# Spacing the tiles of the rounded operands by 2124 and 1100 bytes

## The chip, the cores and the metric

The kernel runs on one core of a Trainium2 chip. The metric is the device time of one launch in microseconds (us), taken as the median of several runs. A profile of one execution stands beside it. Its engines are PE (TensorE, matmuls), PEld (TensorE's loads of the stationary operand), DVE (VectorE), ACT (ScalarE), POOL (GpSimd) and SP (SyncE, which issues the transfers). A number such as L556 is a line of the kernel.

## The reference

For 256 tokens of width 1024 it computes, in float32, two blocks after each other. The first has two layers; each is

```
h = h + 0.5 * swiglu(rms_norm(h, g_ffn1), w_in, w_out)     # hidden width 2816
h = h + mixer(rms_norm(h, g_mix))                          # layer 0: latent attention, layer 1: attention with decay
h = h + 0.5 * swiglu(rms_norm(h, g_ffn2), w_in, w_out)
h = h + sigmoid(rms_norm(h, g_ple) @ w_gate) * (p @ w_proj)
```

with `swiglu(x) = (silu(gate) * up) @ w_out`. The second block is a projection `rms_norm(x) @ w_in` of 3592 columns, short convolutions and a gated delta rule, an output projection, and then 32 experts of width 512, two of them per token:

```
x = x + concat(y_a, y_b) @ w_out
x = x + hier_moe(rms_norm(x), ...)     # silu(x @ w_gate[e]) * (x @ w_up[e]) @ w_down[e]
return rms_norm(x)
```

## The kernel before

**Layout.** Activations lie feature-major: 128 features on the partitions, 8 tiles (`KD`) of 256 tokens. A matmul multiplies a stationary 128x128 tile by a moving operand of 256 or 512 columns into one of eight PSUM banks.

**Products in rounded parts.** TensorE takes plain float32 slowly, and a rounded float32 (`F32R`) faster. The large dense products therefore split both operands into a high part, rounded to `F32R`, and a low part, the rest, and add three products: high by high, low by high, high by low. The helper `three` (L570) does that for one tile. The input of a product lies in `x_parts` (L231): for each k of the 8 tiles the high part `x_hi[:, k]` and right behind it the low part `x_lo[:, k]`, 256 words each. Tile k + 1 follows tile k without a gap, so tiles begin every 2048 bytes. The gate output of a feed-forward layer lies in `act_hi`, `act_lo` and `act` (L236, L251, L252), two buffers each, 1024 bytes apart. The function `inside` (L200) makes these views. It lets all of them begin at word 15 (`INSIDE`) of a flat tensor that is 16 words (`LINE`) longer than it need be, that is at byte 60 of a group of 64; all later tiles begin at byte 60 of their group as well.

```
x_parts = inside(rounded_view("x_parts", [P, 2 * KD * T + LINE]), [P, KD, 2, T])
act_hi = inside(sb("act_hi", [P, 2 * T + LINE], F32R), [P, 2, T])
```

Some tensors share their bytes: `hn` and `sq` lie over `x_parts`, with `behind_hn` between them, `ring_lo` takes the bytes of `ring` itself, and the experts' ring `moe_ring` lies over both and what follows them.

**Weights.** They stream through a ring of four slots of 1.5 MB (`ring`), which SyncE fills in order as slots come free (`ring_free`). ScalarE writes the high parts into `high` or `high_first` (L1524), VectorE subtracts and writes the low parts to `ring_lo` (L2011). All these tiles begin at byte 0 of a group of 64.

**The feed-forward layer** (`gated`, L645, four times) takes 22 chunks of 128 hidden features. For a chunk, `gate_up` (L655) runs 16 matmuls of 512 columns, which take `x_parts[:, k]` whole, high and low side by side, under the high weights, first 8 for gate and then 8 for up; then 16 of 256 columns with `x_hi` under the low weights. `down` (L679) adds the chunk before to the output: 8 output tiles with three matmuls of 256 columns each on `act_hi` and `act_lo`; even chunks use buffer 0 and odd ones buffer 1. Meanwhile ScalarE and VectorE make the gate output of the present chunk (`act_part`, L2076) and split the weights of the next ones. The loop's order is written out by hand, with semaphores between engines.

**Elsewhere.** `x_high_pair` (L1531) and `x_low_pair` (L2037) write `x_hi` and `x_lo`. The second block's input projection (`mix_group`, L996, and the loop over k behind it) uses `three` with `x_hi` and `x_lo` in turn, 28 output tiles by 8. The token products of the attention with decay (`two_units`, L923) turn the roles: the weights move, 512 columns at a time, and `x_hi` and `x_lo` are stationary, 128 columns each. The experts use `act` through `slot_act` (L307), four slots of 128 words. Their weights come through `moe_ring`, twelve places of 1 MB; SyncE's first loads of them wait on `ring_free`, `mix_ready` and `lin_ready`, so for the last dense chunks. All dense matmuls are issued in the helper `mm` and stand under L556, the experts' under L1250.

Of the kernel before, what the change touches and what calls it, by code (L numbers as in the profile page):

```python
# [4 lines left out]


# [1 line left out]

# [1 line left out]

# [4 lines left out]
P = 128  # L15
T = 256
D = 1024
KD = D // P
# [13 lines left out]
QUAD = P // CAP  # L32
# [8 lines left out]
PIECES = 4  # L41
LINE = 16
INSIDE = 15
NEG = -1.0e30

F32 = mybir.dt.float32
F32R = mybir.dt.float32r
# [142 lines left out]
def two_block_kernel(nc, xT, pT, pos, par, weights, experts, out):  # L190
    with ExitStack() as ctx:
        def sb(name, shape, dt=F32):
            return ctx.enter_context(nc.sbuf_tensor("sb_" + name, shape, dt))

        def rounded_view(name, shape):

            with nc.sbuf_tensor("sb_" + name, shape, F32R) as view:
                return view

        def inside(flat, shape):  # L200

            n = math.prod(shape[1:])
            names = "abc"[:len(shape) - 1]
            dims = {a: shape[1 + i] for i, a in enumerate(names)}
            return flat[:, INSIDE:INSIDE + n].rearrange(f"p ({' '.join(names)}) -> p {' '.join(names)}", **dims)

        def sem(name):
            return ctx.enter_context(nc.semaphore(name))
# [2 lines left out]
        params = sb("params", [P, NPAR])  # L211
        narrow = sb("narrow", [P, 16])
        gq, eps_col, peak = narrow[:, 0:4], narrow[:, 4:5], narrow[:, 5:6].bitcast(I32)
        with nc.sbuf_tensor("sb_moe_ring", [P, MOE_RING, MCT * P], F32) as moe_ring:
            pass
        ring_lo = rounded_view("ring_lo", [P, RING, CT * P])
# [11 lines left out]
        v_tok = sb("v_tok", [P, 2, D])  # L228
        oT = sb("oT", [P, KD, T])
        h = sb("h", [P, KD, T])  # L230
        x_parts = inside(rounded_view("x_parts", [P, 2 * KD * T + LINE]), [P, KD, 2, T])  # L231
        x_hi, x_lo = x_parts[:, :, 0, :], x_parts[:, :, 1, :]
        hn = sb("hn", [P, KD, T])
        sb("behind_hn", [P, LINE])
        sq = sb("sq", [P, KD, T])
        act_hi = inside(sb("act_hi", [P, 2 * T + LINE], F32R), [P, 2, T])  # L236
        lnv = sb("lnv", [P, 2, 2 * T])
        rstd = sb("rstd", [P, 2, T])
        pin = sb("pin", [P, 2 * DEPTH, T])
# [8 lines left out]
            pass  # L248
        expg = sb("expg", [P, 2, T])
        gate_r = sb("gate_r", [P, 2, T])  # L250
        act_lo = inside(rounded_view("act_lo", [P, 2 * T + LINE]), [P, 2, T])  # L251
        act = inside(sb("act", [P, 2 * T + LINE]), [P, 2, T])  # L252
        sqh = sb("sqh", [P, 2, 2, T])
        rsh = sb("rsh", [P, 2, 2 * T])
        trig = sb("trig", [P, 4, 2, ROPE // 2])
# [50 lines left out]

        def slot_act(x):  # L307

            return act[:, :, :].rearrange("p a t -> p (a t)")[:, x % QUAD * P:(x % QUAD + 1) * P]
        partial = sq[:, 0:4, :].rearrange("p a t -> p (a t)").rearrange("p (b n) -> p b n", b=2)  # L310
        qkv_pad = scratch[:, 0:12 * PADQ].rearrange("p (n t) -> p n t", t=PADQ)
        u_pad = scratch[:, 12 * PADQ:12 * PADQ + 4 * PADU].rearrange("p (n t) -> p n t", t=PADU)
# [187 lines left out]
        def _(pool):  # L500
# [12 lines left out]
            for i in range(1 - QUAD, QUAD):  # L513
# [5 lines left out]

            st.link(nc.gpsimd.affine_select(out=mask, in_=mask, compare_op=ALU.is_ge, fill=NEG, base=0,  # L520
                                            pattern=[[-1, P]], channel_multiplier=1))
# [30 lines left out]
        def _(pe):  # L552
# [722 lines left out]
            def moe_gathered():  # L1275
# [40 lines left out]
                def down_half(r, p, h, at, pieces=False):  # L1316

                    pe.wait_ge(ex_act, r * QUAD + (2 * p + 2))
                    if not pieces:
                        for e in range(2):  # L1320
                            arrived(r, at + e)
                    for m in (2 * h, 2 * h + 1):
                        for half in range(2):
                            if pieces:
                                pe.wait_ge(last_in[2 * (m % 2) + half], 32)
                            for e in range(2):
                                x = 2 * p + e
                                expert_mm(B[4 + half][CAP * x:CAP * (x + 1), :], slot_act(x)[:, m * CAP:(m + 1) * CAP],
                                     four_tiles(at + e, 8 * (m % 2) + 4 * half), m == 0, m == EC - 1,
                                     (half_down if pieces and not half else ex_down if half else None)  # L1330
                                     if p and e and m == EC - 1 else None)
                    owed_moe[0] += 2
# [664 lines left out]
        def _(dve):  # L1997
# [695 lines left out]
            def R(lo, n):  # L2693
                return route[:, :, lo:lo + n]

            def wide(lo, n):
                return R(lo, 1).to_broadcast([P, 2, n])
# [7 lines left out]
            def by_group(lo):  # L2705
# [14 lines left out]
            V.tensor_tensor(R(40, 4), R(0, 4), wide(36, 4), ALU.subtract).then_inc(rt_max, 1)  # L2720
            st.link(V.scalar_tensor_tensor(out=R(224, 32), in0=R(128, 32), scalar=2.0 * NEG, in1=R(4, 32),
                                           op0=ALU.mult, op1=ALU.add))
# [51 lines left out]
            def moe_gathered():  # L2774
# [21 lines left out]
                def silu_up(r, x):  # L2796
                    s3_, a3 = (v.rearrange("p (m s) -> p m s", s=CAP) for v in (expg[:, 0, 0:P], slot_act(x)))
                    dve.wait_ge(ex_silu, r * QUAD + x + 1)
                    V.tensor_tensor(a3, turned_part(1), s3_, ALU.mult).then_inc(ex_act, 1)  # L2799
# [253 lines left out]
```

## Time and profile before

| | us |
|---|---|
| median of 3 runs | 1723.69 |
| lowest and highest | 1722.62 and 1724.35 |
| the profiled execution, its own time | 1723.16 |
| its span, first to last instruction | 1721.4 |
| TensorE busy | 1615.8 |
| VectorE busy | 987.8 |
| ScalarE busy | 610.3 |

The span is what the profile's views divide up; the execution's own time is 1.8 us longer. Dense products fill the first 1240 us or so, the experts the rest. TensorE's matmuls are pipelined: the busy time of one contains its way through the array, so the pace is the distance from one start to the next.

### The profile page before, as it was taken

Reading aid. Unit: us, or ns where it says so; the run is one execution under the profiler, and the core shown is the slowest. Engines: PE = TensorE matmul, PEld = TensorE weight load, DVE = VectorE, ACT = ScalarE, POOL = GpSimd, SP = SyncE. Lnnn points to the kernel's source line nnn. Section 1 sums busy time; section 2 is a strip of 40 time slices with the busy share of each in tenths; the row PEclk is TensorE's granted clock in tenths of the full one; section 3 lists DMA queues with packets and bytes.
Section 4 is the critical chain, followed back from the end, with each engine's and each line's share of the span. In section 5 each row is a group of like instructions: output and inputs, shape, how many; then the busy total and the mean of one; then the engine's idle time right before and its main releaser. Section 6 shows DMA issues by size and latency. Waiting matters only on the chain.

```text
span 1721.4 us, 25871 instructions
## 1 busy us (share of the span) xinstructions
PE 1615.8 (94%) x10376; PEld 1286.6 (75%) x10376; DVE 987.8 (57%) x1660; ACT 610.3 (35%) x809; POOL 56.4 (3%) x82
## 2 busy tenths in 40 slices
PE   6999999999999999999999999999989788778887
PEld 6999857899998999888889999999954344334333
DVE  7888655687867888865478885787331111111112
ACT  5333346434336333465443334653421000000001
POOL 3000005000000000001100000000000000000000
PEclk9999999999999999999999999999989999999999
DMA  7544441445554555544255555332689999999996
GB/s 279 192 185 183 184 183 74 184 183 190 198 232 158 198 196 184 198 153 164 74 199 200 186 184 220 118 141 74 258 373 425 427 427 427 428 427 427 428 427 271
DMA packets 49240, 415.65 MB, mean 241 GB/s; under 512 B 5616, under 2 KB 5648, under 8 KB 7824
## 3 DMA queue, kind: packets, MB, share of 16 engines
q1 hardware_dynamic: 49104, 414.61, 61.1%
q8 instruction: 51, 0.84, 0.2%
q14 instruction: 21, 0.17, 0.0%
q10 hardware_dynamic: 64, 0.03, 0.0%
HBM read 413.54 MB, written 1.05 MB: 241 GB/s over the span
## 4 chain that ended last, share of the span: by engine, by line
PE 73%; DMA 19%; DVE 4%; ACT 3%; issue 1%; SPq 0%; POOL 0%; DVEq 0%; ACTq 0%
PE bank L556 65%; DMA sb_moe_ring<-experts 18%; PE bank L1250 6%; DVE sb_ring_lo L2011 1%; ACT sb_high L1524 1%; DMA sb_ring<-weights 1%; PE bank L745 0%; PE bank L834 0%; DMA sb_h<-xT 0%; SPq L481 0%; DVE sb_x_parts L2040 0%; ACT sb_high_first L1524 0%; DVE sb_nmax L2144 0%; DVE sb_lnv L2047 0%; ACT sb_x_parts L1535 0%
## 5 line engine op out<-in xcount | busy, mean ns | idle before, releaser
L2011 DVE TENSOR_TENSOR sb_ring_lo<-sb_ring,sb_high 128x2304 fp32r<-128x2304 f32 (+4 forms) x180 | 351.9, 1956 | 123.4 <-ACT sb_high L1524 122.8
L556 PE MATMUL bank<-sb_x_parts,sb_high 128*128 128x512 f32 (+1 forms) x1792 | 407.5, 365 | 0.4 <-DVE sb_ring_lo L2011 0.2
L556 PEld LDWEIGHTS bank<-sb_x_parts,sb_high 128*128 128x128 f32 x1792 | 317.8, 189 | 49.5 <-DVE sb_ring_lo L2011 0.9
L1524 ACT ACTIVATE sb_high<-sb_ring 128x3072 fp32r<-128x3072 f32 x100 | 274.8, 2748 | 139.1 <-PE bank L556 111.0
L556 PE MATMUL bank<-sb_x_parts,sb_ring_lo 128*128 128x256 f32 x1632 | 253.0, 279 | 0.0
L556 PEld LDWEIGHTS bank<-sb_x_parts,sb_ring_lo 128*128 128x128 f32 x1632 | 224.5, 189 | 7.0
L556 PE MATMUL bank<-sb_act_hi,sb_ring_lo 128*128 128x256 f32 x704 | 195.0, 277 | 0.0
L556 PE MATMUL bank<-sb_act_hi,sb_high 128*128 128x256 f32 x680 | 188.6, 277 | 2.2 <-DVE sb_ring_lo L2011 1.7
L556 PE MATMUL bank<-sb_act_lo,sb_high 128*128 128x256 f32 x680 | 187.7, 276 | 0.0
L1250 PE MATMUL bank<-sb_moe_ring,sb_act 128*32 128x512 f32 x512 | 127.4, 643 | 41.2 <-DMA sb_moe_ring<-experts 41.1
L1566 ACT ACTIVATE sb_expg<-sb_gate_r 128x256 f32<-128x256 f32 x88 | 36.7, 417 | 338.0 <-DVE sb_gate_r L2074 337.9
L1250 PE MATMUL bank<-sb_moe_ring,sb_sq 128*32 128x512 f32 x984 | 119.9, 597 | 31.1 <-DMA sb_moe_ring<-experts 30.4
L556 PE MATMUL bank<-sb_oT,sb_ring 128*128 128x256 f32 x640 | 142.8, 379 | 0.0
L556 PEld LDWEIGHTS bank<-sb_oT,sb_ring 128*128 128x128 f32 x640 | 120.7, 190 | 16.7 <-issue 0.8
L556 PEld LDWEIGHTS bank<-sb_act_hi,sb_ring_lo 128*128 128x128 f32 x704 | 131.7, 187 | 0.0
L556 PEld LDWEIGHTS bank<-sb_act_hi,sb_high 128*128 128x128 f32 x680 | 127.2, 187 | 2.6 <-DVE sb_ring_lo L2011 1.9
L556 PEld LDWEIGHTS bank<-sb_act_lo,sb_high 128*128 128x128 f32 x680 | 127.2, 187 | 0.0
L1250 PEld LDWEIGHTS bank<-sb_moe_ring,sb_act 128*32 128x32 f32 x512 | 33.7, 117 | 119.3 <-issue 118.5
L2799 DVE TENSOR_TENSOR sb_act<-bank,sb_expg 128x128 f32<-128x128 f32 x32 | 9.3, 292 | 167.5 <-ACT sb_expg L1952 167.5
L1250 PEld LDWEIGHTS bank<-sb_moe_ring,sb_sq 128*32 128x32 f32 x984 | 28.8, 109 | 96.6 <-issue 92.9
L2794 DVE COPY sb_sq<-bank 128x512 f32<-128x512 f32 x32 | 22.1, 691 | 129.1 <-PE bank L1250 129.1
L1250 PEld LDWEIGHTS bank<-sb_stack,sb_sq 128*128 128x128 f32 x512 | 59.6, 191 | 29.4 <-issue 29.4
(385 smaller groups left out, 1894.5 us busy)
## 6 DMA issues: line engine op xcount, KB each, us to landing
sb_ring<-weights SPq DMA_DIRECT2D x133, 1536.0 KB, 6.5
sb_moe_ring<-experts SPq DMA_DIRECT2D x185, 1024.0 KB, 21.1
sb_qk<-experts SPq DMA_DIRECT2D x4, 1024.0 KB, 15.0
sb_moe_ring<-experts SPq DMA_DIRECT2D x8, 256.0 KB, 17.3
sb_h<-xT SPq DMA_DIRECT2D x2, 512.0 KB, 7.1
sb_ring<-weights SPq DMA_DIRECT2D x2, 512.0 KB, 7.8
sb_oT<-experts SPq DMA_DIRECT2D x1, 1024.0 KB, 15.4
sb_pin<-pT SPq DMA_DIRECT2D x1, 512.0 KB, 17.7
```

The source lines that it names most:

```text
L556: ins = nc.tensor.matmul(o, l, r, start=start, stop=stop, skip_group_check=True)
L1250: ins = nc.tensor.matmul(o, l, r, start=start, stop=stop, skip_group_check=True)
L1524: nc.scalar.activation(high_of(n)[:, lo * P:hi * P], ring[:, n % RING, lo * P:hi * P], ACT.Copy).then_inc(done, 1)
L1566: nc.scalar.activation(expg[:, b, :], gate_r[:, b, :], ACT.Silu).then_inc(sig_ready, 1)
L2011: return V.tensor_tensor(ring_lo[:, n % RING, cols], ring[:, n % RING, cols], high_of(n)[:, cols].bitcast(F32), ALU.subtract)
L2794: V.tensor_copy(partial[:, 1, :], B[1][:, :]).then_inc(part_in[1], 1)
L2799: V.tensor_tensor(a3, turned_part(1), s3_, ALU.mult).then_inc(ex_act, 1)
```

## The change

`inside` now takes a count and a width and leaves 19 words (`STEP`), 76 bytes, behind each tile: x tiles (high and low part together) begin every 2124 bytes and gate-output buffers every 1100. In words within a group of 16, the eight x tiles begin at 15, 2, 5, 8, 11, 14, 1 and 4, the low part of each at the same word as its high part; the two gate-output buffers begin at 15 and 2. The flat tensors grow by 256 or 128 words, and `behind_hn` with them. The room comes from the scratch for transfer descriptors at the start of the memory, which shrinks from its default of 16384 bytes to 1024; 13312 unused bytes (`below_ring`) are laid below the ring. Against before, the tensors from the ring to the start of `x_parts` and `hn` lie 2048 bytes lower, `sq` and `act_hi` 1024, those from `lnv` to `act_lo` and `act` 512, and those behind them where they were. `slot_act` is written for two buffers of two slots. No instruction, wait or semaphore is added or taken away.

```diff
--- before.py
+++ after.py
@@ -5,8 +5,6 @@
 
 
 from contextlib import ExitStack
-
-import math
 
 import numpy as np
 import concourse.bass as bass
@@ -41,6 +39,7 @@
 PIECES = 4
 LINE = 16
 INSIDE = 15
+STEP = 19
 NEG = -1.0e30
 
 F32 = mybir.dt.float32
@@ -197,12 +196,10 @@
             with nc.sbuf_tensor("sb_" + name, shape, F32R) as view:
                 return view
 
-        def inside(flat, shape):
-
-            n = math.prod(shape[1:])
-            names = "abc"[:len(shape) - 1]
-            dims = {a: shape[1 + i] for i, a in enumerate(names)}
-            return flat[:, INSIDE:INSIDE + n].rearrange(f"p ({' '.join(names)}) -> p {' '.join(names)}", **dims)
+        def inside(flat, count, width):
+
+            each = flat[:, INSIDE:INSIDE + count * (width + STEP)].rearrange("p (k n) -> p k n", k=count)
+            return each[:, :, 0:width]
 
         def sem(name):
             return ctx.enter_context(nc.semaphore(name))
@@ -211,6 +208,7 @@
         params = sb("params", [P, NPAR])
         narrow = sb("narrow", [P, 16])
         gq, eps_col, peak = narrow[:, 0:4], narrow[:, 4:5], narrow[:, 5:6].bitcast(I32)
+        sb("below_ring", [P, 26 * P])
         with nc.sbuf_tensor("sb_moe_ring", [P, MOE_RING, MCT * P], F32) as moe_ring:
             pass
         ring_lo = rounded_view("ring_lo", [P, RING, CT * P])
@@ -228,12 +226,12 @@
         v_tok = sb("v_tok", [P, 2, D])
         oT = sb("oT", [P, KD, T])
         h = sb("h", [P, KD, T])
-        x_parts = inside(rounded_view("x_parts", [P, 2 * KD * T + LINE]), [P, KD, 2, T])
+        x_parts = inside(rounded_view("x_parts", [P, 2 * KD * T + LINE + 256]), KD, 2 * T).rearrange("p k (a t) -> p k a t", a=2)
         x_hi, x_lo = x_parts[:, :, 0, :], x_parts[:, :, 1, :]
         hn = sb("hn", [P, KD, T])
-        sb("behind_hn", [P, LINE])
+        sb("behind_hn", [P, LINE + 256])
         sq = sb("sq", [P, KD, T])
-        act_hi = inside(sb("act_hi", [P, 2 * T + LINE], F32R), [P, 2, T])
+        act_hi = inside(sb("act_hi", [P, 2 * T + LINE + 128], F32R), 2, T)
         lnv = sb("lnv", [P, 2, 2 * T])
         rstd = sb("rstd", [P, 2, T])
         pin = sb("pin", [P, 2 * DEPTH, T])
@@ -248,8 +246,8 @@
             pass
         expg = sb("expg", [P, 2, T])
         gate_r = sb("gate_r", [P, 2, T])
-        act_lo = inside(rounded_view("act_lo", [P, 2 * T + LINE]), [P, 2, T])
-        act = inside(sb("act", [P, 2 * T + LINE]), [P, 2, T])
+        act_lo = inside(rounded_view("act_lo", [P, 2 * T + LINE + 128]), 2, T)
+        act = inside(sb("act", [P, 2 * T + LINE + 128]), 2, T)
         sqh = sb("sqh", [P, 2, 2, T])
         rsh = sb("rsh", [P, 2, 2 * T])
         trig = sb("trig", [P, 4, 2, ROPE // 2])
@@ -306,7 +304,7 @@
 
         def slot_act(x):
 
-            return act[:, :, :].rearrange("p a t -> p (a t)")[:, x % QUAD * P:(x % QUAD + 1) * P]
+            return act[:, x % QUAD // 2, x % 2 * P:(x % 2 + 1) * P]
         partial = sq[:, 0:4, :].rearrange("p a t -> p (a t)").rearrange("p (b n) -> p b n", b=2)
         qkv_pad = scratch[:, 0:12 * PADQ].rearrange("p (n t) -> p n t", t=PADQ)
         u_pad = scratch[:, 12 * PADQ:12 * PADQ + 4 * PADU].rearrange("p (n t) -> p n t", t=PADU)
@@ -3043,7 +3041,7 @@
         "pos": np.ascontiguousarray(a["positions"].reshape(2, P).T),
         "par": par, "weights": weights, "experts": experts,
     }
-    nc = bacc.Bacc("TRN2", target_bir_lowering=False, num_devices=1)
+    nc = bacc.Bacc("TRN2", target_bir_lowering=False, num_devices=1, dynamic_dma_scratch_size=1024)
     aps = [nc.dram_tensor(n, v.shape, mybir.dt.from_np(v.dtype), kind="ExternalInput").ap() for n, v in arrays.items()]
     out = nc.dram_tensor("outT", (P, KD, T), F32, kind="ExternalOutput").ap()
     two_block_kernel(nc, *aps, out)
```

## Rows read from the trace of the kernel before

**Rows 1.** The page: the span and the busy time of TensorE (PE) and VectorE (DVE).

```profile
span 1721.4 us, 25871 instructions
PE 1615.8 (94%) x10376; PEld 1286.6 (75%) x10376; DVE 987.8 (57%) x1660; ACT 610.3 (35%) x809; POOL 56.4 (3%) x82
```

**Rows 2.** The page: the chain that ended last, by engine and by line.

```profile
PE 73%; DMA 19%; DVE 4%; ACT 3%; issue 1%; SPq 0%; POOL 0%; DVEq 0%; ACTq 0%
PE bank L556 65%; DMA sb_moe_ring<-experts 18%; PE bank L1250 6%; DVE sb_ring_lo L2011 1%; ACT sb_high L1524 1%; DMA sb_ring<-weights 1%; PE bank L745 0%; PE bank L834 0%; DMA sb_h<-xT 0%; SPq L481 0%; DVE sb_x_parts L2040 0%; ACT sb_high_first L1524 0%; DVE sb_nmax L2144 0%; DVE sb_lnv L2047 0%; ACT sb_x_parts L1535 0%
```

**Rows 3.** Busy time by stretch: us, busy us per engine, PEclk, DMA share, GB/s.

```profile
320.00:600.00 280.00, 278.93 (x1786) 254.47 (x1785) 216.18 (x308) 119.42 (x109) 0.00 (x0) 1.00 0.52 192
...
1240.00:1721.00 481.00, 395.24 (x2579) 197.49 (x2577) 88.06 (x210) 51.94 (x108) 0.00 (x0) 0.96 0.97 408
```

**Rows 4.** TensorE in order of time, one chunk: start us, us, what, how many.

```profile
63.92 3.84 PE L556 MATMUL bank<-sb_x_parts,sb_high 128*128 128x512 f32 x16
67.59 2.03 PE L556 MATMUL bank<-sb_x_parts,sb_ring_lo 128*128 128x256 f32 x16
69.46 0.28 PE L556 MATMUL bank<-sb_act_hi,sb_high 128*128 128x256 f32 x1
69.58 0.28 PE L556 MATMUL bank<-sb_act_lo,sb_high 128*128 128x256 f32 x1
...
72.23 3.83 PE L556 MATMUL bank<-sb_x_parts,sb_high 128*128 128x512 f32 x16
```

**Rows 5.** Groups of instructions by shape: busy us, mean ns, idle before.

```profile
L556 PE MATMUL bank<-sb_x_parts,sb_high 128*128 128x512 f32 x1344 | 322.4, 391 | 0.3 <-DVE sb_ring_lo L2011 0.2
L556 PE MATMUL bank<-sb_x_parts,sb_ring_lo 128*128 128x256 f32 x1632 | 253.0, 279 | 0.0
L556 PE MATMUL bank<-sb_act_hi,sb_ring_lo 128*128 128x256 f32 x704 | 195.0, 277 | 0.0
L556 PE MATMUL bank<-sb_act_hi,sb_high 128*128 128x256 f32 x680 | 188.6, 277 | 2.2 <-DVE sb_ring_lo L2011 1.7 <-DVE sb_act_lo L2091 0.5
L556 PE MATMUL bank<-sb_act_lo,sb_high 128*128 128x256 f32 x680 | 187.7, 276 | 0.0
L556 PE MATMUL bank<-sb_x_parts,sb_high 128*128 128x256 f32 x448 | 85.1, 288 | 0.0
```

**Rows 6.** TensorE in order of time, an output product in whole float32.

```profile
303.74 9.44 PE L556 MATMUL bank<-sb_oT,sb_ring 128*128 128x256 f32 x43
```

**Rows 7.** TensorE in order of time, products of the second block's input projection.

```profile
1160.07 0.40 PE L556 MATMUL bank<-sb_x_parts,sb_high 128*128 128x256 f32 x2
...
1165.02 0.40 PE L556 MATMUL bank<-sb_x_parts,sb_high 128*128 128x256 f32 x2
```

**Rows 8.** TensorE in order of time, token products of the decay attention.

```profile
749.67 0.39 PE L556 MATMUL bank<-sb_ring_lo,sb_x_parts 128*128 128x512 f32 x1
...
755.88 0.39 PE L556 MATMUL bank<-sb_ring_lo,sb_x_parts 128*128 128x512 f32 x1
```

**Rows 9.** VectorE and ScalarE groups: busy us, mean ns, idle before.

```profile
L2085 DVE TENSOR_TENSOR sb_act<-sb_act,sb_expg 128x256 f32<-128x256 f32 x84 | 35.7, 425 | 6.2 <-ACT sb_expg L1566 0.9
L2074 DVE TENSOR_TENSOR sb_gate_r<-sb_gate_r,sb_rstd 128x256 f32<-128x256 f32 x88 | 37.4, 425 | 3.0
L1535 ACT ACTIVATE sb_x_parts<-sb_h,sb_params 128x256 fp32r<-128x256 f32 x48 | 21.3, 495 | 11.9 <-DMA sb_h<-xT 6.0 <-DVE sb_h L2004 3.5 <-DVE sb_h L2188 2.3
L1617 ACT ACTIVATE sb_oT<-sb_h,sb_params 128x256 f32<-128x256 f32 x16 | 6.6, 497 | 5.4 <-DVE sb_h L2004 5.4
```

**Rows 10.** DMA issues: KB each, median us from issue to landing.

```profile
sb_ring<-weights SPq DMA_DIRECT2D x133, 1536.0 KB, 6.5
sb_moe_ring<-experts SPq DMA_DIRECT2D x185, 1024.0 KB, 21.1
```

## The prediction, made before the change was run

> **What bounds the kernel now.** The page first: TensorE is busy for 94% of the span [rows 1], and 73% of the chain that ended last is TensorE's, 65% of the span at L556, the line of the dense products [rows 2]. The busy share alone proves nothing, so the stretches come next. From 320 to 600 us, a feed-forward layer almost throughout, TensorE is busy 278.93 of 280 us at a granted clock of 1.00 (the 2.4 GHz level), VectorE 216.18, ScalarE 119.42, and the transfers take half of their engines. After 1240 us, among the experts, the DMA share is 0.97: there the stream of weights sets the pace [rows 3]. So in the dense part nothing but TensorE's own pace counts, and what it gains there moves the start of the experts' stream and the end with it, because that stream's first loads wait for the last dense chunks.
>
> The pace is read from starts, not from the duration of one matmul, which contains its latency. In one chunk [rows 4] 16 matmuls of 512 columns start between 63.92 and 67.59 us: 3.67/16 = 229.4 ns each. The 16 of 256 columns on x take 1.87/16 = 116.9 ns, the 24 of the down product 2.77/24 = 115.4 ns. At 2.4 GHz the columns alone are 213.3 and 106.7 ns. Matmuls on plain float32, two cycles per column here, start every (9.44 - 0.38)/42 = 215.7 ns for 256 columns [rows 6] (0.38 us is the length of one), which is 2.4 ns over 213.3. So the rounded operands lose 16.1 ns per 512 columns and 10.2 or 8.7 ns per 256, where 2.4 would be enough. The loss grows with the columns: (229.4 - 116.9) = 112.5 ns for 256 more, 5.8 over 106.7. What reads four bytes in each cycle stumbles; what reads them every other cycle doesn't. That is the loss which an address could change, and the only thing in this profile that the edit can reach.
>
> **The change part by part.** Counts come from the loops. Seven of eight x tiles and one of two gate outputs begin elsewhere; tile 0 and buffer 0 stay 60 bytes into their group of 64. In the four feed-forward layers x is read by 4 x 22 x 16 = 1408 matmuls of 512 and 1408 of 256 columns (7/8: 1232 each), the gate output by 4 x 22 x 24 = 2112 (half: 1056). The second block's input projection reads x in 224 x 3 = 672 matmuls of 256 (588). The attention's 288 token products have x as the stationary operand (252).
>
> Does the place of a tile matter at all? Three rows say a little. The gate output's lower part, at 276 ns, is the shortest of the 256-column forms; the upper part has 277, x 279 [rows 5]. In the input projection the same three-matmul pattern as in the down product, with high, high and low weights in turn, runs at (1165.02 - 1160.07)/42 = 117.9 ns, against 115.4 in the down product [rows 4, 7]. All begin 60 bytes into 64, but the gate output's two parts lie in different tensors and x's two parts end to end. So the relation of one read to the next costs up to 2.5 ns, and the new spacing changes that relation.
>
> Terms, each taken as far as the best pace that the trace shows:
> - x at 256 columns in the layers: 1232 x (116.9 - 115.4) = 1.8 us less.
> - x in the input projection: 588 x (117.9 - 115.4) = 1.5 us less.
> - gate output: two of three forms by the 1 ns between 277 and 276 would be 1056 x 2/3 = 0.7 us; I take 0.5 less.
> - x at 512 columns: no row shows a better pace. I take half of the 1.5 ns of the first term, since two tiles' halves are read in one run and only the joint between tiles changes: 1232 x 0.75 = 0.9 us less.
> - x as stationary operand: its load ends well inside the 230 ns of the 512 columns beside it [rows 8]: nothing; with a bound of 1.5 ns either way, 0.4 us.
>
> Bounds. Below: all four groups fall to 2.4 ns over their columns (215.7 and 109.1): 1232 x 13.7 + 1232 x 7.8 + 588 x 8.8 + 1056 x 6.3 = 16.9 + 9.6 + 5.2 + 6.7 = 38.4 us less. Above: each moved matmul outside the projection pays the 2.5 ns by which the worst pattern stands over the best: (1232 + 1232 + 1056) x 2.5 = 8.8 us more. The value taken lies near the small end because all rows of like width lie within 2.5 ns of each other.
>
> What goes at nothing. The writers: VectorE takes 425 ns for 256 columns into the gate output at 60 bytes and 425 into the aligned gate tile; ScalarE 495 ns into x, 497 into an aligned tile [rows 9]. They don't see the place, and VectorE has some 60 us of slack in 280 besides [rows 3]. The matmuls of the experts that read the gate output lie under the stream with its DMA share of 0.97. The other tensors move by 2048, 1024 or 512 bytes or not at all, so none changes its place in a group of 64 or 512; the weights' transfers keep whole rows of the same size, and their 6.5 us lie within the 4 x 8.31 us in which their four slots go round [rows 4, 10]. No instruction, wait or semaphore is added. The smaller descriptor scratch serves transfers that GpSimd would issue; here all large ones are SyncE's.
>
> Sum: 1.8 + 1.5 + 0.5 + 0.9 = 4.7 us less. The profiled execution took 1723.16 us (span 1721.4 and 1.8 around it), so 1718.5; the median of the runs is 0.5 above it: **1719.0 us**. A measurement of this kernel can tell some 0.2%, 3.4 us, from no change; on 4108 moved moving operands that is 0.84 ns or two cycles each.
>
> **Rivals.**
> - **Nothing changes** (1723.7). For it: the attention's token products stream weights' tiles that begin at byte 0 of a group, and 27 of them take 755.88 - 749.67 = 6.21 us, 230.0 ns each [rows 8], no better and no worse than x with its 60 bytes at 229.4. If 0 and 60 are alike, 8, 20 or 32 may be too, and the loss is the reader's own rhythm. Against it: the 2.5 ns between patterns of equal width. The Trainium skill, page "TensorE: Matmul & The Clock Gate", section "Back-to-back issue gap", has N/2.4 plus 2.5 ns and no address in it; the float32 row agrees with it, the rounded rows don't. The page "SBUF — State Buffer" speaks of 16-byte lines with a penalty for each access that crosses into a new one; a run of 512 neighbours crosses some 128 wherever it begins, so by that rule too nothing moves.
> - **Much of the loss goes** (about 1708). If the stumble comes of every tile beginning at one place, spread places remove it, wholly 38 us, by 0.4 of it 15. For it: the loss is seen only where reads are fastest. Against it: it grows with the columns inside one matmul, while the edit moves only starts.
> - **Slower** (1732.5). Now x tile k+1 begins at the very next word behind tile k, in a group just read; 76 bytes of gap end that, and each start opens a fresh group. If that costs what the input projection pays over the down product, the bound above holds: 8.8 us more. It decides from 0.84 ns per matmul on. For it: the pattern that jumps back within x, in the projection, is the slowest. Against it: the gate output jumps between tensors at every matmul and is the fastest.
> - That the change doesn't do what it says: the views are plain, and each tile stays contiguous, so I give this nothing of its own.
>
> **How the numbers follow.** Small gain 0.42, no change 0.36, much of the loss 0.09, slower 0.13. Of the small gain a tenth falls within 0.2%, as its 4.7 us is close to 3.4. Faster: 0.38 + 0.09 = 0.47; same: 0.36 + 0.04 = 0.40, less a little that slips to the slow side: 0.38; slower 0.15. The range goes down to 1709 and up to 1727, and leaves out most of the large gain and the worse half of the slow case. The small gain's own range is 1716 to 1721.
>
> **What would show it.** In the changed profile: the 16 matmuls of 512 columns in 3.66 us or less, the 16 of 256 in 1.85, the projection's 42 in 4.85, a chunk in under the present 72.23 - 63.92 = 8.31 us; half of the down products as before. The writers' 425 and 495 ns unchanged. I am wrong if the chunk stays at 8.31 us, if it grows, or if the time goes or comes in the experts' part, which the edit shouldn't reach.

## The result and the profile after the change

The changed kernel takes 1737.83 us (median of 6 runs, 1736.83 to 1738.75), against 1723.87 for the kernel before in the same comparison (6 runs, 1722.62 to 1724.35). The ratio is 1.0083, with a 95% interval of 1.0072 to 1.0093: 14 us slower. That is the side that the forecast gave 0.15, and it lies outside the range. The profiled execution took 1738.75 us, 15.6 more than the one of before.

The page of the kernel after: span, busy time by engine, and the chain that ended last by engine.

```profile
span 1737.0 us, 25871 instructions
PE 1638.2 (94%) x10376; PEld 1296.9 (75%) x10376; DVE 987.6 (57%) x1660; ACT 611.0 (35%) x809; POOL 56.7 (3%) x82
...
PE 76%; DMA 17%; DVE 3%; ACT 2%; issue 1%; SPq 0%; POOL 0%; DVEq 0%; ACTq 0%
```

Instructions are as many as before, and only TensorE's busy time grows: 22.4 us more, VectorE, ScalarE and GpSimd within 0.7 us [rows 1]. TensorE's share of the chain goes from 73 to 76% [rows 2].

The busy times by stretch of the kernel after (columns as in [rows 3]):

```profile
320.00:600.00 280.00, 279.10 (x1750) 252.84 (x1749) 213.50 (x305) 120.14 (x115) 0.00 (x0) 1.00 0.52 192
1240.00:1737.00 497.00, 417.12 (x2646) 211.53 (x2644) 92.30 (x216) 59.60 (x118) 0.00 (x0) 0.95 0.95 400
```

Dense TensorE is as full as before and at the same granted clock of 1.00, but starts 1750 matmuls in 280 us where it started 1786: the same work, each piece slower. The experts' part isn't where it went: by the starts in the traces, the first matmul on an expert's tile comes at 1268.6 us before and at 1283.4 after, the last at 1706.5 and at 1721.9. Of the 15.6 us, 14.8 are there before the stream of experts' weights is first read.

TensorE in order of time, one chunk and the next, after:

```profile
65.10 3.90 PE L554 MATMUL bank<-sb_x_parts,sb_high 128*128 128x512 f32 x16
68.83 2.07 PE L554 MATMUL bank<-sb_x_parts,sb_ring_lo 128*128 128x256 f32 x16
70.74 0.28 PE L554 MATMUL bank<-sb_act_hi,sb_high 128*128 128x256 f32 x1
...
73.62 3.89 PE L554 MATMUL bank<-sb_x_parts,sb_high 128*128 128x512 f32 x16
77.34 2.07 PE L554 MATMUL bank<-sb_x_parts,sb_ring_lo 128*128 128x256 f32 x16
79.25 0.28 PE L554 MATMUL bank<-sb_act_hi,sb_high 128*128 128x256 f32 x1
...
82.05 3.90 PE L554 MATMUL bank<-sb_x_parts,sb_high 128*128 128x512 f32 x16
```

The 16 of 512 columns take 3.73 us (233.1 ns each, 229.4 before), the 16 of 256 columns 1.91 (119.4 against 116.9), the 24 of the down product 2.88 and 2.80 (120.0 and 116.7 against 115.4), and a chunk 8.52 or 8.43 in place of 8.31 [rows 4]. The two chunks differ because the gate output's two buffers now begin at different places.

The second block's input projection, after, 36 matmuls apart (the three of a group in turn):

```profile
1175.15 0.28 PE L554 MATMUL bank<-sb_x_parts,sb_ring_lo 128*128 128x256 f32 x1
...
1179.43 0.28 PE L554 MATMUL bank<-sb_x_parts,sb_ring_lo 128*128 128x256 f32 x1
```

4.28/36 = 118.9 ns, 117.9 before [rows 7]. The groups of the kernel after (busy us, mean ns, idle before):

```profile
L554 PE MATMUL bank<-sb_x_parts,sb_high 128*128 128x512 f32 x1344 | 327.2, 395 | 0.2 <-DVE sb_ring_lo L2009 0.2
L554 PE MATMUL bank<-sb_act_hi,sb_high 128*128 128x256 f32 x680 | 191.1, 281 | 1.9 <-DVE sb_ring_lo L2009 1.5 <-DVE sb_act_lo L2089 0.4
L554 PE MATMUL bank<-sb_act_lo,sb_high 128*128 128x256 f32 x680 | 190.5, 280 | 0.0
L2083 DVE TENSOR_TENSOR sb_act<-sb_act,sb_expg 128x256 f32<-128x256 f32 x84 | 35.8, 426 | 6.2 <-ACT sb_expg L1564 0.9
L1533 ACT ACTIVATE sb_x_parts<-sb_h,sb_params 128x256 fp32r<-128x256 f32 x48 | 21.3, 496 | 12.1 <-DMA sb_h<-xT 6.3 <-DVE sb_h L2002 3.5 <-DVE sb_h L2186 2.3
```

Each matmul is 4 ns longer; the writers are not (426 and 496 ns, 425 and 495 before [rows 5, 9]).

The rest of this text goes by **start to start**, in TensorE cycles at 2.4 GHz (the granted clock is 1.00 there), each a mean over the matmuls of its kind that didn't wait for anything, worked out from the starts in a kernel's trace. For the kernels before and after:

| kind, count | before | after | more time |
|---|---|---|---|
| x, 512 columns, 1408 | 551.0 | 559.4 | 4.9 us |
| x, 256 columns, 1408 | 279.8 | 285.8 | 3.5 us |
| gate output: upper/high, lower/high, upper/low weights, 704 each | 278.2, 276.1, 278.0 | 284.3, 285.5, 281.1 | 5.5 us |
| input projection, 672 | 282.4 | 286.2 | 1.1 us |
| token products, x stationary, 288 | 552.4 | 558.3 | 0.7 us |

The sum is 15.7 us, the profiled executions' difference 15.6: nothing else is needed. What had to be found is why a start at another word costs that.

### The profile page after: what moved, and what is told of

Same layout as the page of the kernel before. It is cut to its first block, busy times and chain, and to the rows that moved or that the text cites. A ratio compares the mean times of both kernels' runs of the same rounds, so it can differ in the third digit from the quotient of the medians.

```text
span 1737.0 us, 25871 instructions
## 1 busy us (share of the span) xinstructions
PE 1638.2 (94%) x10376; PEld 1296.9 (75%) x10376; DVE 987.6 (57%) x1660; ACT 611.0 (35%) x809; POOL 56.7 (3%) x82
## 4 chain that ended last, share of the span: by engine, by line
PE 76%; DMA 17%; DVE 3%; ACT 2%; issue 1%; SPq 0%; POOL 0%; DVEq 0%; ACTq 0%
PE bank L554 69%; DMA sb_moe_ring<-experts 17%; PE bank L1248 6%; DVE sb_ring_lo L2009 1%; ACT sb_high L1522 1%; PE bank L743 0%; PE bank L832 0%; DMA sb_h<-xT 0%; SPq L479 0%; ACT sb_high_first L1522 0%; DVE sb_nmax L2142 0%; DVE sb_x_parts L2038 0%; ACT sb_expg L1622 0%; PE bank L952 0%; ACT L1479 0%
## 5 line engine op out<-in xcount | busy, mean ns | idle before, releaser
L554 PE MATMUL bank<-sb_x_parts,sb_high 128*128 128x512 f32 (+1 forms) x1792 | 413.1, 369 | 0.3 <-DVE sb_ring_lo L2009 0.2
L1522 ACT ACTIVATE sb_high<-sb_ring 128x3072 fp32r<-128x3072 f32 x100 | 275.5, 2755 | 144.4 <-PE bank L554 116.7
L554 PE MATMUL bank<-sb_x_parts,sb_ring_lo 128*128 128x256 f32 x1632 | 257.0, 283 | 0.0
L1248 PE MATMUL bank<-sb_moe_ring,sb_act 128*32 128x512 f32 x512 | 134.9, 675 | 41.0 <-DMA sb_moe_ring<-experts 40.9
```

The source lines that it names most:

```text
L554: ins = nc.tensor.matmul(o, l, r, start=start, stop=stop, skip_group_check=True)
L1248: ins = nc.tensor.matmul(o, l, r, start=start, stop=stop, skip_group_check=True)
L1522: nc.scalar.activation(high_of(n)[:, lo * P:hi * P], ring[:, n % RING, lo * P:hi * P], ACT.Copy).then_inc(done, 1)
```

## The experiments

Four causes were open, three of them forms of **A**: the address sets the pace of a rounded matmul, either **(A1a)** each place with a price of its own, **(A1b)** by how it differs from the one read before, or **(A2)** because the joint between neighbouring tiles is gone. The fourth is **B**: the other tensors that moved, or the smaller descriptor scratch. Addresses are told below as 4-byte words within 64 (256 bytes), counted from where the weights' tiles begin; x begins at word 15 of its group throughout the kernel before. Where only INSIDE, STEP, a tensor's spacing or its first word is edited, the rest is the changed kernel, with the flat tensors and the unused bytes sized to fit.

**The spacing undone, the rest kept** (INSIDE stays 15):

```diff
-STEP = 19
+STEP = 0
```

> The changed kernel with STEP = 0: tiles joined again at 2048 and 1024 bytes, all else of the change kept (smaller scratch, below_ring, longer tensors, new addresses). Theory A (the spacing costs, whatever part of it): back to the kernel before, 1723.9 us within 2, with 229.6 ns per matmul of 512 columns and 116.7 per 256. Theory B (the moved tensors cost, by 2048, 1024 or 512 bytes): stays at 1738 us within 2.

1723.45 us, ratio 0.9994 (0.9985 to 1.0004), and the cycles of the kernel before to 0.1. So B is out: the moved tensors, the views and the scratch cost nothing that can be measured.

**A gap of 64 bytes: the joint is lost, the place in each 64 bytes is not.**

```diff
-STEP = 19
+STEP = 16
```

> STEP = 16: a gap of 64 bytes behind each tile, so every tile begins at byte 60 of its group of 64, but no tile joins the one before. Theory A1 (the differing places within a group of 64 cost): 1724 us within 2, the 16 matmuls of 512 columns at 229.6 ns each. Theory A2 (the lost joint costs, my slower rival: each start opens a fresh group): 1738 us, about 232.7 ns per 512 columns.

**The same gap, all tiles 8 bytes into their 64:**

```diff
-INSIDE = 15
-STEP = 19
+INSIDE = 2
+STEP = 16
```

> STEP = 16 and INSIDE = 2: every tile begins at byte 8 of its group of 64, all alike. Theory A1a (each place has its own price, and byte 60 is the cheap one): slower than before, by at least the 14 us of the change. Theory A1b (only a difference between one tile's place and the next's costs): 1724 us within 2. Theory A2: 1738 us as with any gap.

Measured: 1727.21 us, 1.0013 (1.0004 to 1.0023), some 3 us more than before and just above what A1 allowed, and 1746.33 us, 1.0127 (1.011 to 1.0144). TensorE in order of time with the 64-byte gap at word 15:

```profile
64.45 3.83 PE L554 MATMUL bank<-sb_x_parts,sb_high 128*128 128x512 f32 x16
68.12 2.04 PE L554 MATMUL bank<-sb_x_parts,sb_ring_lo 128*128 128x256 f32 x16
```

The 16 of 512 columns take 3.67 us, just what they took joined: the lost joint doesn't cost 14 us, so A2 is out as the main cause. The second kernel has the same gap and the same sameness, since each tile is alike within its 64 bytes, and is the slowest yet (563.7 and 288.6 cycles): a place has a price, A1a. But with the gap the four starts 15, 31, 47 and 63 aren't all alike either: 256 columns rose from 279.8 to 282.0. That speaks for a group larger than 64 bytes; the table further down shows it.

**Matmuls alone.** This kernel leaves the whole computation out: it rounds x into one tensor for the moving and one for the stationary operand and runs 64 matmuls of each pattern. In the first patterns 8 tiles lie 528 words apart, each at word p of its 64 bytes.

```diff
+for p in range(16):
+    add("wide_" + LET[p], 512, flat(p), tiles(0))
...
+for name, pitch in (("joined", 512), ..., ("gapf", 576), ("gapg", 640)):
+    add("wide" + name, 512, flat(15, pitch), tiles(0, 128))
```

> Leaves the computation out: 64 matmuls on rounded operands for each of 90-odd settings of the start of the moving tile (word 0 to 15 of a group of 16), of the stationary tile, of two alternating starts, and of the spacing, at 256 and 512 columns. Theory A1a: the pace depends on the start with all tiles alike (sets wide, half), with word 15 among the cheapest, by 1 to 4 ns. Theory A1b: wide and half are flat over the 16 starts, and only the alternating sets (alt, widealt) rise above them. Theory A2: the joined sets are 3 ns faster than gapc (64 bytes), and nothing else matters.

TensorE in order of time, 64 matmuls in a line (the pattern's name, not a tensor of the kernel, is the output):

```profile
801.60 14.86 PE L87 MATMUL o_widejoined<-sb_moving,sb_weights 128*128 128x512 f32 x64
816.29 7.66 PE L87 MATMUL o_halfgapa<-sb_moving,sb_weights 128*128 128x256 f32 x64
...
935.26 14.67 PE L87 MATMUL o_widegapf<-sb_moving,sb_weights 128*128 128x512 f32 x64
949.77 7.63 PE L87 MATMUL o_halfgapg<-sb_moving,sb_weights 128*128 128x256 f32 x64
```

Joined tiles: (816.29 - 801.60)/64 = 229.5 ns, 551 cycles, the kernel's own 551.0. With 256 bytes between them (gapf): 14.51/64 = 226.7 ns, 544 cycles, and the same with 512 bytes or with one tile read again and again. The first matmuls of a pattern often start at another pace than the rest, so the cycles given for bare patterns, here and below, are of the settled pace: without the first seven or eight. Over the 16 starts the price runs from 548 to 575 cycles for 512 columns and from 276 to 292 for 256, though each of these patterns stays at one place within its 64 bytes: A1b as the only cause is out. Alternating between two places isn't free, however. At 256 columns word 11 in turn with word 15 costs 284.1 cycles, where either by itself costs 276.0, and over the 15 alternating patterns the mean is 285.0, against 280.9 for the mean of the two places; at 512 columns none of the eight is above 564. The changed kernel's own pitch of 531 words gives 557.4 and 287.9 here, against 559.4 and 285.8 in the kernel. So an effect of this size is there without any other engine or transfer.

**One tensor's spacing at a time.**

```diff
-STEP = 19
+X_STEP = 19
+GATE_STEP = 0
```

> Only x spaced by 2124 bytes, gate output joined again. By the starts in the changed kernel's trace x accounts for 1408 x 3.1 ns (512 columns) + 1408 x 2.3 (256) + 672 x 1.5 (projection) + 0.7 us (token products) = 9.4 us of the 14: 1733 us within 2. If the gate output alone were at fault: 1724; if the parts depended on each other the two runs wouldn't add up to 14.

```diff
-STEP = 19
+X_STEP = 0
+GATE_STEP = 19
```

> Only the gate output spaced by 1100 bytes, x joined again. By the starts in the changed kernel's trace it accounts for 5.4 us of the 14: 1729 us within 2.

1734.52 us, 1.0062 (1.0045 to 1.0079), and 1727.19 us, 1.0021 (1.0011 to 1.003): 10.4 and 3.1 us over the 1724.08 of the kernel before there, 13.5 together, against 14.0 for both. The x-only kernel has after's 560.3 and 285.8 cycles on x, and 280.4, 279.4, 279.3 on the untouched gate output, 2 cycles more than before on average. What was read before these products matters to them, then; more on that below.

**x with 256 bytes between tiles, all at word 15; gate output as before:**

```diff
-STEP = 19
+X_STEP = 64
+GATE_STEP = 0
```

> x tiles 2304 bytes apart (a gap of 256 bytes), all at byte 60 as before, gate output joined. In the run of the bare matmuls this spacing took 226.7 ns per 512 columns against 229.6 joined, and 116.7 at 256 columns in both. If the same holds here, 1408 x 2.9 ns = 4.1 us less than before: 1719.8 us, the only candidate so far for beating both kernels. If only the place within a group of 64 counted: no change, 1723.9.

```profile
71.33 3.79 PE L555 MATMUL bank<-sb_x_parts,sb_high 128*128 128x512 f32 x16
74.96 2.03 PE L555 MATMUL bank<-sb_x_parts,sb_ring_lo 128*128 128x256 f32 x16
76.82 0.28 PE L555 MATMUL bank<-sb_act_hi,sb_high 128*128 128x256 f32 x1
```

The 16 of 512 columns take 3.63 us here in place of 3.67, and over the kernel 544.8 cycles, the 544 of the bare pattern. 1721.34 us, 0.9987 (0.9977 to 0.9996): 2.7 us less, where 1408 x 6.2/2.4 is 3.6. What the prediction hoped to find in the joint is there, but it needs tiles that stay at one good place.

**A price for each word.** Again matmuls alone, 24 of a pattern, one moving and one stationary tile, the moving one at each word, and one set with the stationary tile moved.

```diff
+for width, name in ((256, "half_"), (512, "wide_")):
+    for d in range(128):
+        out.append((name + LET[d // 16] + LET[d % 16], width, lambda i, d=d: d, lambda i: 0))
```

> Leaves the computation out: 24 matmuls on one and the same moving tile and one and the same stationary tile, for starts of the moving tile at words 0 to 127 (256 and 512 columns) and of the stationary tile at words 0 to 63. Theory A1a in its simple form: a table that repeats every 16 words and has word 15 among its lowest. Theory C (what costs is how moving and stationary reads lie to each other over a longer distance, and how one tile's end lies to the next's start): with a single repeated pair the 512-column pace stays within 2 ns of 226.7 for all starts, or repeats only over 64 words or more.

TensorE in order of time, one line for each start (aa is word 0, ab word 1, ap word 15, ba word 16, ea word 64):

```profile
566.85 5.84 PE L68 MATMUL o_wide_ab<-sb_moving,sb_weights 128*128 128x512 f32 x24
572.53 5.75 PE L68 MATMUL o_wide_ac<-sb_moving,sb_weights 128*128 128x512 f32 x24
...
645.12 5.61 PE L68 MATMUL o_wide_ap<-sb_moving,sb_weights 128*128 128x512 f32 x24
650.57 5.66 PE L68 MATMUL o_wide_ba<-sb_moving,sb_weights 128*128 128x512 f32 x24
...
919.05 5.61 PE L68 MATMUL o_wide_ea<-sb_moving,sb_weights 128*128 128x512 f32 x24
924.50 5.84 PE L68 MATMUL o_wide_eb<-sb_moving,sb_weights 128*128 128x512 f32 x24
...
1002.77 5.61 PE L68 MATMUL o_wide_ep<-sb_moving,sb_weights 128*128 128x512 f32 x24
1008.22 5.66 PE L68 MATMUL o_wide_fa<-sb_moving,sb_weights 128*128 128x512 f32 x24
```

Word 1 costs (572.53 - 566.85)/24 = 236.7 ns, 568 cycles; word 15 costs 227.1, 545; and words 64 and 79 are words 0 and 15 again. Over all starts the price repeats after 64 words, 256 bytes, and not before. The table of 512 columns, cycles, words 0 to 15 in the first line:

```
546 568 560 549 556 576 560 544 560 563 560 552 560 560 560 544
549 568 566 548 554 560 560 556 560 565 552 560 556 568 563 552
560 576 560 555 560 560 564 544 562 568 560 552 560 571 560 552
560 576 560 555 563 572 564 552 560 567 560 544 544 576 552 544
```

Its columns show what the rows of before couldn't: words 3, 7, 11 and 15 of each 16 are cheap (544 to 560, 550 on average), words 1, 5, 9 and 13 dear (560 to 576, 568 on average); the others stand between (557 and 560), but words 0 and 60 are as cheap as any. For 256 columns the prices run from 272 to 295. Word 15 of the first line is one of the cheapest in the table. That is the kernel before; the change spreads x over words 15, 34, 53, 8, 27, 46, 1 and 20, whose mean is 559.8, and 286.8 for 256 columns. The changed kernel's trace has 559.4 and 285.8. The stationary tile's word moves the price of 256 columns between 277 and 288 too.

**The table tried in the kernel: x at word 7 and at word 1** (256-byte gaps, gate output as before):

```diff
-x_parts = inside(rounded_view("x_parts", ...), KD, 2 * T, X_STEP)
+x_parts = inside(rounded_view("x_parts", ...), KD, 2 * T, X_STEP, 7)
```

> As the run with x 2304 bytes apart, but all x tiles begin at word 7 instead of 15 of their 64 words. Theory D (each start within 256 bytes has its own price, as in the table of single pairs: word 15 is 544 cycles at 512 columns and 280 at 256, word 7 is 544 and 277): as before at 512 columns, 1.1 ns less at 256: 1.5 us below that run, 1719.8 us. If only byte 60 of 64 is cheap: slower than before, 1730 or more.

```diff
+x_parts = inside(rounded_view("x_parts", ...), KD, 2 * T, X_STEP, 1)
```

> The same with word 1, which the table of single pairs gives 568 cycles at 512 columns and 294 at 256, the highest price. Theory D: 236.7 ns per 512 columns and 122.5 per 256, so 1408 x 9.9 + 1408 x 5.8 + 672 x 5 ns = 25 us above the run with word 15, 1747 us, though no tile's start differs from another's. Theory A1b (differences between starts cost): 1721 us.

Word 1: 1746.01 us, 1.0133 (1.0116 to 1.015). Its first chunk's lines:

```profile
72.94 3.95 PE L555 MATMUL bank<-sb_x_parts,sb_high 128*128 128x512 f32 x16
76.73 2.12 PE L555 MATMUL bank<-sb_x_parts,sb_ring_lo 128*128 128x256 f32 x16
78.68 0.29 PE L555 MATMUL bank<-sb_act_hi,sb_high 128*128 128x256 f32 x1
```

3.79 and 1.95 us where word 15 took 3.63 and 1.86 with the same gaps. Over the kernel 568.4 and 292.8 cycles, 567.9 and 294.4 in the table. Every tile at one place, and 25 us slower than word 15: the price is the place's, not the spread's. Word 7: x at 544.8 and 277.3 cycles, 544 and 277.3 in the table, but 1722.88 us, 0.9997 (0.9988 to 1.0007), not the gain expected. The gate output, which was not touched, went from 277.7 to 282.5 cycles on average: 2112 x 4.8/2.4 = 4.2 us, more than the 1.8 that x gained (1408 x 2.4/2.4 and 672 x 1.4/2.4). With the token products' 8.2 cycles (1.0 us) the means make 3.4 us over the kernel at word 15, where the two profiled executions differ by 1.5; the rest of that difference I can't place.

**Groups of three, as the down product runs them**, matmuls alone, both parts at one word or 16 words apart, and the stationary tile at words 4 and 32:

```diff
+for gap in (0, 16):
+    for a in range(64):
+        b = (a + gap) % 64 + 1024
+        out.append((two("triple" + LET[gap // 16], a), 256, lambda i, a=a, b=b: (a, b, a)[i % 3],
+                    lambda i: (0, 0, 1024)[i % 3] + i // 3 * 128))
```

> Leaves the computation out: 24 matmuls each for the down product's pattern (high, low, high on two moving tiles that both begin at word 0 to 63, or 16 words apart), for single pairs at 512 columns with the stationary tile begun at word 4 and at word 32, and for eight tiles in a row joined or 256 bytes apart, begun at word 0 to 15. Theory D, if the price is that of the moving start's address: the 512-column tables for stationary word 4 and 32 equal the one for 0. If it is that of the distance between the two: they are the same table moved by 4 and 32 words. Joined tiles cost 2 to 8 cycles more than those apart at word 15; at other words the theory doesn't say.

TensorE in order of time, stationary tile at word 32, moving at words 0, 1 and 2 (aa, ab, ac), then 32, 33 and 34 (ca, cb, cc):

```profile
741.44 5.76 PE L77 MATMUL o_widei_aa<-sb_moving,sb_weights 128*128 128x512 f32 x24
747.04 5.92 PE L77 MATMUL o_widei_ab<-sb_moving,sb_weights 128*128 128x512 f32 x24
752.79 5.77 PE L77 MATMUL o_widei_ac<-sb_moving,sb_weights 128*128 128x512 f32 x24
...
920.60 5.61 PE L77 MATMUL o_widei_ca<-sb_moving,sb_weights 128*128 128x512 f32 x24
926.05 5.84 PE L77 MATMUL o_widei_cb<-sb_moving,sb_weights 128*128 128x512 f32 x24
931.73 5.75 PE L77 MATMUL o_widei_cc<-sb_moving,sb_weights 128*128 128x512 f32 x24
```

Words 32 and 33 now cost 5.45/24 and 5.68/24 us, 545 and 568 cycles, which were the prices of words 0 and 1; and words 0 and 1 cost 560 and 575, those of words 32 and 33. The table has moved by 32 words with the stationary tile. With that tile at word 4 it isn't the table moved by 4, so more than the distance counts. In threes, the parts where the kernel before has them (words 31 and 47) cost 277.3 cycles on average, and its trace has 277.4; the changed kernel's second buffer (words 50 and 2) costs 286.3, the mean of the two 281.8, and the kernel with only the gate output's spacing has 282.2. The cheapest, 272.0, are both parts at word 4, 28, 36 or 48.

**The gate output at those words**, x at word 15 with 256-byte gaps:

```diff
-act_hi = inside(sb("act_hi", ...), 2, T, GATE_STEP)
-act_lo = inside(rounded_view("act_lo", ...), 2, T, GATE_STEP)
+act_hi = inside(sb("act_hi", ...), 2, T, GATE_STEP, 20)
+act_lo = inside(rounded_view("act_lo", ...), 2, T, GATE_STEP, 4)
```

> x 2304 bytes apart at word 15 as in the fastest run so far; the gate output's high and low tiles both at word 36 of their 64 (before: 31 and 47). The table of triples gives 272.0 cycles against the 277.3 of 31 and 47. Theory D: 2112 x 2.2 ns = 4.7 us below that run, 1717 us. Theory E (the pace carries over from the matmuls before): the down product takes something between 272 and 284, 1716 to 1726 us.

(first words 20 and 4 put both at word 36 of their 64, as the tensors lie; 32 and 16 put them at word 48)

> The same with both gate-output tiles at word 48, for which the table gives 272.0 cycles too. Theory D: 1717 us. Theory E: another value than at word 36, between 1716 and 1726.

The same as the first, with x at word 7:

> Gate output at word 36 and x at word 7. Theory D: x at 544 and 277 cycles, gate output at 272: 1.5 us below the run with x at 15 and gate output at 36, 1715.5 us. Theory E: the down product is slower than with x at word 15, as it was with the old gate words (282.5 against 277.7): 1720 us or more.

Measured: 1728.83 us, 1.0028 (1.0018 to 1.0039), slower than either expectation; **1716.84 us, 0.9961 (0.9948 to 0.9974)**; and 1726.12 us, 1.0014 (1.0004 to 1.0023). The chunk with the gate output at word 36:

```profile
73.00 3.79 PE L555 MATMUL bank<-sb_x_parts,sb_high 128*128 128x512 f32 x16
76.64 2.03 PE L555 MATMUL bank<-sb_x_parts,sb_ring_lo 128*128 128x256 f32 x16
78.50 0.28 PE L555 MATMUL bank<-sb_act_hi,sb_high 128*128 128x256 f32 x1
...
81.38 3.79 PE L555 MATMUL bank<-sb_x_parts,sb_high 128*128 128x512 f32 x16
```

and at word 48:

```profile
74.95 2.03 PE L555 MATMUL bank<-sb_x_parts,sb_ring_lo 128*128 128x256 f32 x16
76.81 0.28 PE L555 MATMUL bank<-sb_act_hi,sb_high 128*128 128x256 f32 x1
...
79.54 3.80 PE L555 MATMUL bank<-sb_x_parts,sb_high 128*128 128x512 f32 x16
```

The products on x are the same in both; the down product takes 2.88 us at word 36 and 2.73 at word 48, 120.0 and 113.8 ns each. Word 48 keeps its price in the kernel (272.0 to 273.2 cycles for the three forms), word 36 doesn't: 287.7 with x at word 15, 285.5 with x at word 7, against 272.0 when it ran alone. The kernel at word 48 beats both the one before, by 6.8 us, and the changed one.

**What carries over.** The traces show the pace inside the down product, from its first start to its last. Cycles, means over the chunks:

| kernel | first matmul | 1 to 8 | 9 to 16 | 17 to 24 |
|---|---|---|---|---|
| before (gate output at 31 and 47) | 278 | 277 | 277 | 277 |
| only x spaced by 2124 bytes | 292 | 284 | 278 | 277 |
| x at word 1 | 301 | 288 | 278 | 277 |
| x at word 7 | 284 | 283 | 283 | 283 |
| gate output at word 36 | 284 | 288 | 288 | 288 |
| gate output at word 48 | 282 | 273 | 272 | 272 |

The first four rows have the gate output at the same words. Behind spread x tiles, or x at word 1, the products begin up to 22 cycles dearer and come down to the pace of before; that is the 2 cycles of the x-only kernel. Behind x at word 7 they never come down, and at word 36 they go to 288 at the second matmul and stay. So the same places can have more than one steady pace.

**What stays open.** A price measured by a pattern that runs alone holds for x in the layers of the six kernels compared, to within 3 cycles, and for the gate output at word 48, at the places of before and at those of after to within 2. It fails at word 36, and the untouched gate output changes by up to 5 cycles with x's word. What chooses between the steady paces, and why a start has its price at all, no run here shows.

## Why the prediction was wrong

**The step that failed** is the bound of the unknown place: the four terms for moved tiles, 4.7 us less in all, where the starts show 15.0 more (and 0.7 more for stationary x, put at nothing). The prediction took the pace of the best other pattern of equal width for what a moved tile would reach, and said that "the relation of one read to the next costs up to 2.5 ns, and the new spacing changes that relation". Rows 4, 5 and 7 were all taken at starts that the tables put among the cheap ones for their pattern: 15 for x, and 31 with 47 for the gate output, the cheapest that parts 16 words apart have. Their spread of 2.5 ns was the spread among good places. It said nothing of the 32 cycles, 13.3 ns per 512 columns, between the best word and the worst, and the edit moved tiles from the good end to places all over.

Point by point:
- **x at 512 columns**, 0.9 us less: 4.9 more. The joint does cost 7 cycles, as half suspected, and 256-byte gaps at word 15 gave 6.2 of them back. The change removes the joint and loses 15 to the new words, 8.4 in all. By the rival's bound this would have been 2.5 ns per moved matmul; it was 8.4/2.4 x 8/7 = 4.0.
- **x at 256 columns**, 1.8 less: 3.5 more. **Projection**, 1.5 less: 1.1 more. That x in the projection was slower than the gate output in the same pattern was read as a relation between neighbouring reads; by the bare threes about half of it is the place: 280.0 cycles at word 15 and 277.4 at 31 and 47, where the kernel has 282.4 and 277.4. The other half no run accounts for.
- **Gate output**, 0.5 less: 5.5 more, of which the kernel with this edit alone has 2112 x (282.2 - 277.4)/2.4 = 4.2 (3.1 by the medians); the rest came with x's spacing. The bound above was 1056 x 2.5 = 2.6 us.
- **Stationary x**, nothing with a bound of 0.4: 0.7 more, 5.9 cycles each, though its load takes 189 ns, 188 before. So the stationary tile's word is part of the price and not its load's length; with x at word 7 these products cost 560.7 cycles.
- **The rival "slower"** had the right sign and the right point of decision, but the wrong mechanism (the lost joint and a fresh group at each start) and so a bound of 8.8 us that the result passed. The gap alone, tiles at word 15 of each 64 bytes, cost 3.
- **"Nothing changes"** argued that bytes 0 and 60 cost alike (230.0 and 229.4 ns [rows 4, 8]). They do: 546 and 544 in the table. Two places alike were taken to speak for the other fourteen. The Trainium skill, page "TensorE: Matmul & The Clock Gate", section "Back-to-back issue gap", gives an isolated gap of N/2.4 + 2.5 ns, an estimate of 215.8 ns for 512 columns with no address in it; the runs have 226.7 to 240. The Trainium skill, page "SBUF — State Buffer", section "Specifications (TRN2)", has lines of 16 bytes, by which, as an estimate, every fourth word should be alike; the table's period is 64 words, though the word within 16 bytes does sort the cheap starts from the dear on average.
- **Right**: that only TensorE's pace between starts counts, the counts of matmuls, the writers' times, within 1 ns, that of the edit nothing but the spacing matters (shown by the undone spacing), that the experts' part adds almost nothing (0.8 us), and that a chunk's starts would show it.

The range failed with the bound: its upper end of 1727 stood on the 8.8 us, while x alone has a good and a bad word 25 us apart.

## What to carry to other kernels

When an edit moves a rounded operand, the spread among rows of the old kernel bounds nothing, for they may all sit at good places: measure the bare matmul at each start before it is costed, price each moved tile by its new start less its old one, and take the dearest and the cheapest start as the bounds. In a stream bound by TensorE, put each moving tile at one measured start in its 256 bytes, with gaps that keep it there, rather than spread them. Then try it in the kernel, for a price measured alone can fail behind other matmuls: of two starts of the gate output with the same 272 cycles alone, one made a kernel 6.8 us faster than before and the other one 5.2 us slower.

## What the runs showed of the hardware

- A matmul of 128 by 128 on rounded float32 starts every 544 to 576 cycles with 512 moving columns (226.7 to 240 ns at 2.4 GHz) when one pattern runs alone, and every 272 to 295 with 256, by the moving tile's first word within 256 bytes; no start reached 2.4 ns over its columns, which plain float32 has at 256 [rows 6].
- In the table for a stationary tile at word 0, words 3 modulo 4 are the cheapest on average (550 cycles) and words 1 modulo 4 the dearest (568). Moving the stationary tile by 32 words moves the table by 32; by 4 it changes it.
- Tiles read end to end at word 15 cost 551 cycles, with 256 bytes between them 544; at word 9 it is 574 and 563, at word 0 both are 544.
- A change of x's start moved the pace of products on another, untouched tensor by up to 5 cycles of 278 on average, in two cases by up to 22 at first and back to 277 over some 12 matmuls, in one for all 24.
